# Column quarters per 32 tokens in the expert passes of a streaming encoder layer, with VectorE transposes, 16 KB weight rows and a one-hot token table

## What is computed

```python
def expert_ffn(xb, w_gu, b_gu, w_dn, b_dn):
    gu = xb @ w_gu + b_gu
    gate = jnp.minimum(gu[..., :D_FF], SWIGLU_LIMIT)
    up = jnp.clip(gu[..., D_FF:], -SWIGLU_LIMIT, SWIGLU_LIMIT)
    glu = gate * jax.nn.sigmoid(gate * SWIGLU_ALPHA)
    return ((up + 1) * glu) @ w_dn + b_dn
```

## Time and profile before

| | us |
|---|---|
| median of three runs | 1817.5 (1816.2 to 1819.22) |
| profiled execution, its own time | 1819.62 |
| span of its trace | 1817.8 |
| TensorE busy | 1570.0 (86%) |
| VectorE busy | 701.1 (39%) |
| ScalarE busy | 323.9 (18%) |
| POOL busy | 155.7 (9%) |
| mean granted TensorE clock | 0.901 |

### The profile page before, as it was taken

The page is one execution under the profiler, slowest core; times in us unless marked ns, Lnnn a source line. Parts: engine busy times, 40 slices in busy tenths (PEclk is TensorE's granted clock), DMA queues, the critical chain, the costliest instruction groups (busy, mean ns, idle before and its releaser), DMA issues.

```text
span 1817.8 us, 39267 instructions
## 1 busy us (share of the span) xinstructions
PE 1570.0 (86%) x16465; PEld 750.6 (41%) x16465; DVE 701.1 (39%) x1414; ACT 323.9 (18%) x678; POOL 155.7 (9%) x241
## 2 busy tenths in 40 slices
PE   3998888789992299999999999999999999999920
PEld 2664754555652044344443433433433433433400
DVE  1379996433346022232222222222222222222248
ACT  2231116333321011111111111111111111111001
POOL 1024104000111300000000000000000000000031
PEclk8898998655995599999999999999999999999965
DMA  9235548000444579999999999999999999997763
GB/s 346 77 106 186 186 172 300 1 4 3 151 177 156 205 310 408 402 407 401 408 406 399 396 400 390 392 403 393 391 402 392 388 409 391 393 402 272 306 249 109
DMA packets 129291, 531.20 MB, mean 292 GB/s; under 512 B 12634, under 2 KB 22156, under 8 KB 95444
## 3 DMA queue, kind: packets, MB, share of 16 engines
q1 hardware_dynamic: 100112, 472.07, 66.4%
q0 software_dynamic: 12272, 41.28, 6.9%
q10 hardware_dynamic: 16852, 17.11, 2.8%
HBM read 501.04 MB, written 29.37 MB: 292 GB/s over the span
## 4 chain that ended last, share of the span: by engine, by line
PE 50%; DMA 36%; DVE 6%; ACT 3%; issue 2%; POOL 1%; ACTq 1%; SPq 0%; DVEq 0%; POOLq 0%
DMA down_w<-in_w_down 32%; PE psum L1712 9%; PE psum L1694 8%; PE psum L1720 6%; PE psum L1515 5%; PE psum L1703 4%; PE psum L1653 3%; PE psum L1619 2%; PE psum L1523 2%; PE psum L1634 2%; DMA front_ring<-in_w_in 1%; DVE final_work L1277 1%; PE psum L1494 1%; PE psum L1627 1%; POOL slot_dram L1420 1%
## 5 line engine op out<-in xcount | busy, mean ns | idle before, releaser
L1712 PE MATMUL psum<-down_w,expert_work 128*32 128x512 f32 x2112 | 240.0, 595 | 17.2 <-DMA down_w<-in_w_down 17.2
L1694 PE MATMUL psum<-gu_even,expert_work 128*32 128x512 f32 x2176 | 239.1, 597 | 1.3 <-ACT expert_work L824 1.0
L1215 DVE TENSOR_TENSOR expert_work<-psum,expert_work 128x512 f32<-128x512 f32 x66 | 36.8, 558 | 500.6 <-PE psum L1694 372.1
L1694 PE MATMUL psum<-gu_odd,expert_work 128*32 128x512 f32 x2048 | 222.7, 592 | 0.0
L1233 DVE TENSOR_TENSOR expert_work<-psum,expert_work 128x512 f32<-128x512 f32 x66 | 36.9, 558 | 303.0 <-PE psum L1712 214.9
L1694 PEld LDWEIGHTS psum<-gu_even,expert_work 128*32 128x32 f32 x2176 | 70.9, 111 | 159.4 <-issue 156.8
L1712 PEld LDWEIGHTS psum<-down_w,expert_work 128*32 128x32 f32 x2112 | 63.0, 109 | 155.2 <-issue 120.1
L1694 PEld LDWEIGHTS psum<-gu_odd,expert_work 128*32 128x32 f32 x2048 | 66.6, 110 | 146.3 <-issue 143.6
L1703 PE MATMUL psum<-gu_even,expert_work 128*32 128x256 f32 x2176 | 124.0, 380 | 0.0
L1720 PE MATMUL psum<-down_w,expert_work 128*32 128x256 f32 x2112 | 120.0, 379 | 0.0
L1703 PE MATMUL psum<-gu_odd,expert_work 128*32 128x256 f32 x2048 | 116.8, 380 | 0.0
(11 more groups left out here) (308 smaller groups left out, 1616.9 us busy)
## 6 DMA issues: line engine op xcount, KB each, us to landing
gu_even<-in_w_gate_up SPq DMA_DIRECT2D x68, 2048.0 KB, 22.7
down_w<-in_w_down SPq DMA_DIRECT2D x66, 2048.0 KB, 23.3
gu_odd<-in_w_gate_up SPq DMA_DIRECT2D x64, 2048.0 KB, 22.9
front_ring<-in_w_mod SPq DMA_DIRECT2D x12, 2048.0 KB
ys_dram<-raw_ring POOLq DMA_DIRECT2D x1, 8448.0 KB, 39.3
ys_dram<-expert_work ACTq DMA_DIRECT2D x66, 128.0 KB, 7.2
front_ring<-in_w_in SPq DMA_DIRECT2D x4, 2048.0 KB
front_ring<-in_w_mod_final SPq DMA_DIRECT2D x4, 2048.0 KB
```

What stands on the lines that cost most here:

```text
L1215: v.tensor_tensor(eg[part], psum[:, 2 * part, 0:w], bias_of(bias_b, part, 0), ALU.add).then_inc(gu_added, 1)
L1694: last = mm(psum[32 * u:32 * u + 32, x, :], lhsT=xgT[:, k, 32 * g_:32 * g_ + 32], rhs=gu_slot(par, c)[:, k % 2, at_:at_ + WA], start=(k == ...
L1712: last = mm(psum[32 * u:32 * u + 32, 4, :], lhsT=actT[0][:, at_:at_ + 32], rhs=dn_slot(c)[:, k % 4, n * WA:(n + 1) * WA], start=(k == 0), ...
```

## The change

- The 96 tokens of a pass are three groups of 32, each as four column quarters of 256 (`gate_up` L1686, `down` L1694). For each gate/up piece TensorE takes the three groups in turn; then down for one group after another. Groups 0 and 2 share a PSUM bank for down, so group 2 waits for group 0's `rows_out`.
- The transposes are VectorE's: of tokens (L1196, 128x768) and of activations (L1213, 128x256), with weight rows laid out as `(p k)` to match: a partition's part of any 2 MB piece is one row of 16 KB.
- Tokens come by three indirect transfers of 128 rows of 1 KB (`h_quarters`). Bias loads are two instead of six, the shuffle is 768 wide.
- A pass has three stores, one per group (L814), each of 128 rows of 1 KB. `ys_dram` is seen there as quarter, token, column.
- The token table is made on the chip's engines: one-hot rows of group and place (VectorE L1175, L1178), 20 matmuls 128x153 that sum them (L1675), one drain (L1187). `slot_dram` goes.
- An overflow pass does one group of 32. gu_odd's first load no longer waits for the routing. ScalarE loads the sigmoid table once.

The core of the diff:

```diff
-        w_gu = a["w_gate_up"][0].rearrange("e (k p) n -> e p k n", p=P)
-        w_dn = a["w_down"][0].rearrange("e (k p) n -> e p k n", p=P)
+        w_gu = a["w_gate_up"][0].rearrange("e (p k) n -> e p k n", p=P)
+        w_dn = a["w_down"][0].rearrange("e (p k) n -> e p k n", p=P)
...
-            def store_rows(b):
-                act_e.wait_ge(ys_ready, 2 * b + 3)
-                for n in range(2):
-                    act_e.dma_start(ys_dram[bass.ds(b * ROWS_B, 64), n * WA:(n + 1) * WA],
-                                    ysb[0][64 * n:64 * n + 64, :]).then_inc(ys_stored, 16)
-                act_e.wait_ge(ys_ready, 2 * b + 4)
-                for u in range(GROUPS):
-                    act_e.dma_start(ys_dram[bass.ds(b * ROWS_B + 64, 32), u * WB:(u + 1) * WB],
-                                    ysb[1][32 * u:32 * u + 32, :]).then_inc(ys_stored, 16)
+            def store_rows(n, g_):
+                act_e.wait_ge(ys_ready, n + GB + 1)
+                act_e.dma_start(ys_dram[bass.ds(n * GT, GT), :].rearrange("t (u n) -> u t n", u=QUARTERS),
+                                ysb[g_]).then_inc(ys_stored, 16)
...
+                    for tt in range(T):
+                        cols = slice(TOPE * tt, TOPE * (tt + 1))
+                        v.tensor_tensor(at_group[:, cols, :], iota_g.unsqueeze(1).to_broadcast([P, TOPE, NG]),
+                                        f6[:, cols].unsqueeze(2).to_broadcast([P, TOPE, NG]), ALU.is_equal)
+                        for c in range(TOPE * tt, TOPE * (tt + 1)):
+                            ins = v.tensor_scalar(at_row[:, c, :], iota_r, f3[:, c:c + 1], tok4[:, tt:tt + 1], ALU.is_equal, ALU.mult)
+                        ins.then_inc(hot_made, 1)
...
+                elif kind == "table":
+                    for tt in range(T):
+                        pe.wait_ge(hot_made, tt + 1)
+                        rws = ROWS[tt]
+                        for c in range(TOPE * tt, TOPE * (tt + 1)):
+                            last = mm(bank(j)[:, 0:NG], lhsT=at_row[0:rws, c, :], rhs=at_group[0:rws, c, :],
+                                      start=(c == 0), stop=(c == T * TOPE - 1))
...
+            def turn_tokens(b, par):
+                dve.wait_ge(gathered, (b + 1) * (GB * 16))
+                dve.sem_inc(turn_settled, 1)
+                v.transpose(xgT[par].rearrange("p g k n -> p (g k) n"),
+                            xg.rearrange("p (g f k) -> p g k f", g=GB, k=KD)).then_inc(xgT_ready, 1)
...
+            def expert_dve(b, par):
+                turn_tokens(b + 1, 1 - par)
+                dve.wait_ge(bias_ready, b + 1)
+                for g_ in range(GB):
+                    if g_ < GB - 1:
+                        dve.wait_ge(gu_ready, b * (GB - 1) + g_ + 1)
+                    else:
+                        dve.wait_ge(gu_done, (b + 1) * GUC)
+                    gated(b * GB + g_, g_)
+                dve.wait_ge(ys_stored, (b + 1) * (GB * 16))
+                for g_ in range(GB):
+                    if g_ < GB - 1:
+                        dve.wait_ge(dn_ready, b * (GB - 1) + g_ + 1)
+                    else:
+                        dve.wait_ge(dn_done, (b + 1) * DNC)
+                    rows_out(b * GB + g_, g_)
+                spread_bias(b + 1, (b + 1) * GB)
...
+            def expert_pe(b, par, use_gu, groups, n):
+                for c in range(GUC):
+                    pe.wait_ge(gu_in[par][c], use_gu * 16 + 16)
+                    for g_ in range(groups):
+                        last = gate_up(g_, par, c, xgT[par])
+                        if g_ == groups - 1:
+                            last.then_inc(gu_done, 1)
+                        elif c == GUC - 1:
+                            last.then_inc(gu_ready, 1)
+                for g_ in range(groups):
+                    pe.wait_ge(actT_ready, n + g_ + 1)
+                    if g_ != 1:
+                        pe.wait_ge(ys_ready, n + GB + g_ // 2)
+                    for c in range(DNC):
+                        if g_ == 0:
+                            pe.wait_ge(dn_in[c], b * 16 + 16)
+                        last = down(g_, c)
+                        if g_ == groups - 1:
+                            last.then_inc(dn_done, 1)
+                    if g_ < groups - 1:
+                        last.then_inc(dn_ready, 1)
```

More of the change, by code:

```diff
@@ L123, in steps @@
             s.append(("hT", t + 1))
-    s += [("rank",)]
+    s += [("rank",), ("table",), ("over",)]
     return s
@@ L1237, in spread_bias, with rows_out @@
+            def rows_out(n, g_):
+                v.tensor_tensor(ysb[g_], down_sum(g_), bias_b[:, 2 * QW:3 * QW], ALU.add).then_inc(ys_ready, 1)
+            def spread_bias(b, rows_before):
+                dve.wait_ge(ys_ready, rows_before + GB)
                 dve.wait_ge(bias_in, (b + 1) * (BIAS_DMAS * 16))
@@ L1438, in expert_pool @@
-            def expert_pool(b):
-                pool.wait_ge(xg_turned, b + 1)
-                gather(b + 1)
-            gather(0)
+                for g_ in range(n):
+                    g.indirect_dma_start(xg[:, g_ * QW:(g_ + 1) * QW], None, h_quarters,
+                                         bass.IndirectOffsetOnAxis(idx_now[:, g_:g_ + 1], 0)).then_inc(gathered, 16)
+            in_sbuf(pool, ("table",))
+            gather(0, GB, 0)
             with pool.Fori(0, NE) as b:
-                expert_pool(b)
+                pool.wait_ge(xgT_ready, b + 1)
+                settle()
+                gather(b * GB + GB, GB, b + 1)
@@ L1698, in gate_up_rest @@
-            def gate_up_rest(par, c):
+                elif kind == "table":
+                    for tt in range(T):
[4 more added lines that the diff above has]
+                                      start=(c == 0), stop=(c == T * TOPE - 1))
+                elif kind == "over":
+                    pe.wait_ge(routed, 1)
+                    last = tr(bank(j)[0:1, 0:P], ocol, ident)
@@ L1743, in _, with down @@
-            in_sbuf(pe, ("rank",))
+                        for u in range(QUARTERS):
+                            last = mm(psum[GT * u:GT * u + GT, 2 * g_ + x, 0:QW], lhsT=xT[:, g_, k, :],
+                                      rhs=gu_slot(par, c)[:, k % 2, x * D + u * QW:x * D + (u + 1) * QW],
+                                      start=(k == 0), stop=(k == KD - 1))
+                return last
+            def down(g_, c):
+                for k in range(4 * c, 4 * c + 4):
+                    for u in range(QUARTERS):
+                        last = mm(down_sum(g_)[GT * u:GT * u + GT, :], lhsT=actT[g_][:, k, :],
+                                  rhs=dn_slot(c)[:, k % 4, u * QW:(u + 1) * QW], start=(k == 0), stop=(k == KD - 1))
+                return last
```

361 lines of the change are left out of this document (140 added, 221 removed).

## The result

| | before | changed |
|---|---|---|
| median, us | 1818.36 (1816.2 to 1819.78, 4 runs) | 1850.34 (1837.74 to 1855.36, 4 runs) |
| profiled execution, us | 1819.62 | 1837.74 |
| its span, us | 1817.8 | 1835.8 |
| start of the first expert matmul, us | 626.66 | 589.60 |
| middle passes, us each | 33.7 | 35.9 |

The change is slower: ratio 1.0167, 95% interval 1.0114 to 1.0219. The forecast was 1912 us. The time lies under the forecast's own range of 1885 to 1990 and inside the stated one only because rival 1 takes that down to 1805; the forecast growth of 94 us was three times the measured 32. The profiled execution is the fastest of the four, 12.6 us under their median, so its rows show a little less waiting than the middle one would.

The account below looks back on a forecast made before the run. The prediction took TensorE and the DMA engines as both at their limit in the experts' stage. 1817.5 - 20.7 (start) + 115.7 (passes) - 0.9 (tail) gave 1912 us; own range 1885 to 1990, low end 1805 with rival 1.

Parts of the forecast that it names:

- rival 1: Stores on four engines without the gap: they land early, only the engines' 35.5 us a pass counts; 1828 us, chance 0.16.
- Four engines for a store: Stores whose DRAM side begins with 4 column quarters use 4 engines, not 16; each gets 96 store rows a pass.
- TensorE's pass: TensorE's matmuls in a pass: 192 + 96 of 256 columns, with the ends of accumulations, take 31.4 us.
- The activation chain: Seven steps on VectorE and ScalarE per group, 3.3 us, hidden under 3.46 us of gate/up matmuls.
- A 16 KB row: Weight transfers: such a row holds its engine for 0.61 us, bounds 0.60 and 0.64.
- 34 store rows: Store rows gone per engine before weights flow again; 62 remain against 48 weight rows, so stores always land last.
- the period of 38.4 us: Time of each of 29 passes: 35.5 us of engine load plus a 3.1 us gap, less 0.2.
- the margin of 14: Store rows by which the remaining 62 exceed the next pass's 48 weight rows on the four engines.
- the term of 115.7 us: Growth of all passes together, overflow pass included: 1226.5 us against 1110.8.
- The start: Token table made on chip: expert matmuls start at 606 us, bounds 599 and 612, instead of 626.66; -20.7 us.
- the engines' own load of 35.5 us: Weight rows, 96 store rows, gathers, bias and completions on each of the four store engines, per pass.
- The rival on the other side: Stores run on all 16 engines, passes take 31.4 to 32.0 us: 1709 to 1726 us, up to 1770; chance 0.12.

Follow-up runs that it names:

- e10: The kernel before with the change's form of store (one transfer for the 64 rows, one for the 32) in place of six: 1972.66 us, ratio 1.0844.
- e3: The change with stores split by column quarter into 12 transfers a pass and TensorE's loop written out: 1728.78 us, ratio 0.949 to the kernel before.
- e1: The change with each store split into its four column quarters, 12 transfers a pass in place of 3: 1814.37 us, ratio 0.9971 to the kernel before.
- e4: The change with a second set of output buffers, a semaphore each, stores still on 4 engines: 1817.89 us, ratio 0.9986 to the kernel before.
- e5: The change with every 2 MB weight piece loaded as two transfers of 8 KB rows: 1818.95 us, ratio 1.0002 to the kernel before.
- e2: The change with TensorE's loop over pairs of passes written out 16 times: 1856.38 us, ratio 1.02 to the kernel before.
- e9: The change as it is, run once more for its spread: 1849.02 us, ratio 1.0179 to the kernel before.
- e8: The kernel before with four passes in TensorE's loop body in place of two: 1857.71 us, ratio 1.0223.
- e7: The change with two sets of output buffers and TensorE's loop written out, stores on 4 engines: 1841.24 us, ratio 1.0138 to the kernel before.
- e6: The change with stores split by column quarter, TensorE's loop written out and weights in 8 KB rows: 1740.28 us, ratio 0.9572 to the kernel before.

## Why the prediction was wrong

**What held.** Four engines for a store (18040 packets here, and e10). TensorE's pass: 31.3 us against 31.4. The activation chain is hidden: in e3 TensorE waits for nothing but down pieces, though the transposes take 655 and 1571 ns where I had 350 to 1000 and 1200. A 16 KB row is 0.61 us when nothing disturbs it (below). The direction, the mechanism (`rows_out` held by stores, TensorE's third down group behind it) and the turns row by row hold too (e1, e4, e5). The arithmetic of the range does not: the bounds named there add up to 1891 to 1998 us, not 1885 to 1990.

**The step that failed** is "By then some 34 store rows are gone; 62 remain, against 48 weight rows. So the stores always land last", and the period of 38.4 us for each of 29 passes. DMA queues of the change from 762 to 769 us, right behind the landing at 761.63, with q1 alone from 763 to 767 us as the third row; then from 769 to 776 us; then from 733 to 761 us, before that landing:

```profile
q1 hardware_dynamic: 65, 1.06, 42.4%
q10 hardware_dynamic: 264, 0.26, 12.9%
...
q1 hardware_dynamic: 16, 0.26, 26.1%
...
q1 hardware_dynamic: 199, 3.00, 100.5%
...
q1 hardware_dynamic: 674, 9.45, 87.1%
...
q10 hardware_dynamic: 287, 0.28, 2.9%
```

Right behind the landing 264 packets of q10 went out, which is 2 stores of 128 rows and 4 completions each: the stores of groups 0 and 1, all of them, 64 rows an engine and not 34. All had gone by 767, and until then q1 had started only 16 packets of weights. Only group 2's 32 rows stay for the next pass, and against 48 weight rows they land in time. (The fourth row is weights undisturbed: 3.00 MB are 183 rows, at 100.5% of 16 engines for 7 us 0.61 us each. The last two are stores under weights: 9.45 MB are 36 weight rows an engine in the mean, beside 72 store packets for each of the four, in 28 us.) That pass waits for nothing, its own stores are issued under weights, and the pass after it waits.

Two terms of that step were off. Store rows began to flow between 763 and 764 us, some 2 us after the landing, where I had 3.1. And the third down group, which frees the down pieces, was taken at 3.5 us; it took 5.35 us after 3.75 us of idle, at a lower granted clock (the 0.66 in this window, 762 to 767 us):

```profile
762.00:767.00 5.00, 4.87 (x60) 2.67 (x64) 0.41 (x2) 0.00 (x0) 0.00 (x0) 0.66 0.39 105
```

SP issued the first down load at 764.93, in the middle of that group. As an estimate, half of the extra 1.85 us gives the stores 0.9 us, or some 18 rows at 0.05 us, which alone is more than the margin of 14. No run separates the two terms: behind a third group at full clock (3.66 us) the next pass waited once (1483.23) and once did not (831.85).

The period is one of two passes. e2 shows it alone: 31.1 + 42 = some 73 us for two, 36.5 a pass, in place of 76.8. So 29 x (38.4 - 36.5) = 55 us of the term of 115.7 us are this error, by the period that e2 shows.

**What I hadn't seen** is the stop at the head of TensorE's loop. A timeline row and a window of the change:

```profile
658.58 4.05 PE L1686 MATMUL psum<-gu_even,expert_work 128*32 128x256 f32 x34 [4.74 <-issue]
...
947.00:950.00 3.00, 3.00 (x36) 1.61 (x35) 0.00 (x0) 0.00 (x0) 2.39 (x3) 0.59 0.98 416
```

4.74 us of idle before the matmul of an even pass, and the granted clock afterwards at 0.59 in the mean of 3 us, between the levels of 1.2 and 2.4 GHz: 1.9 us more for the same matmuls (22.61 against 20.72). That is 3.3 us a pass. Beside late stores it costs nothing that shows, since stores land in it: the change is at 35.9 (e9 36.3) with it, at 36.5 without (e2). With the stores mended it costs the whole: 34.7 against 32.1 us (e1, e3), 86 us of time. The loop's 15 returns go with 166 more packets of 16 KB in the instruction queue than before; e2, which never returns, has 137 more for 9216 matmuls, about 243 B each. By this estimate the body was 100 KB before, is 140 KB in the change and 200 KB in e8, and the bound lies between the first two. The Trainium skill, Runtime: NRT & Kernel Launch, section "Instruction fetch mechanics", gives TensorE a store of 128 KiB, refilled in blocks of 16 KiB, and says that a taken branch to code outside the current window of two pages has to fetch first. These runs agree with the 128 KiB: no stop at 100 KB, stops at 140 and 200. They don't agree with a window of only two blocks, which the 100 KB body would have left as well.

**The start.** I had 606 us, it was 589.60. The chain of the change (answers to the earlier trace rows):

```profile
561.17 0.87 PE psum L1666 x2
...
579.29 1.32 PE psum L1675 x8
...
585.07 2.69 DMA expert_work<-h_dram,keep
...
589.60 10.49 PE psum L1686 x161
```

From the rank matmuls to the first expert matmul it is 28.4 us, before 626.66 - 572.19 = 54.5 (the first rank matmul there, just ahead of the one in the earlier trace rows): the table gains 26 us, I had 20.7. Most of what was off is the series of table matmuls, 1.32 us for four (each leaves two records, so the row says x8), 0.33 each, where I took 0.6; they end 0.4 us behind VectorE's last one-hots. The other 11 us lie ahead of the change's work: in the twelve profiled executions of this study the first rank matmul stands anywhere from 561.2 to 574.9 us, and in those of the changed kernel and its variants at either end. So the profiled execution was an early one, by luck, and this is a part of the spread of 1%.

**The sum again**, for the profiled execution: -37 us for the start, passes from 589.60 to some 1754 = 1164 us against 1110.8, which is +54, tail +1: 1817.8 + 18 = 1835.8. The median of the change, 12.6 us above this execution, has no profile of its own; e9's profiled execution, at 1848.59 us, starts at 593.23 with 36.3 us a pass and eleven waits for `rows_out`, 41.8 us in all. Of my rivals the first came nearest (1828), but by another way: the engines' own load of 35.5 us with stores that land early. e4 shows passes of 34.65 us with the same load, so 35.5 was at least 0.8 too high (0.61 x 48 + 96 x 0.046 + 6 x 0.16 is 34.7; the gathers run as 96 packets of 4 KB a pass, 6 an engine, and not as 384 rows of 1 KB), and the stores do land late. The rival on the other side, 1709 to 1726 us with 16 engines, is what e3 reaches (1729), once the loop's stop is gone too.

## What to carry to other kernels

Read the outermost count of a transfer on both sides: here 4 in place of 32 or 64 put 3% of the traffic on four of 16 engines, and up to every second pass waited. A loop body that grows can cost its engine a stop at each return, which shows as idle time "issue" at its head and as packets in the instruction queue. When two waits fill the same time, each edit alone shows little (36 us gained and 6 lost here, 121 gained together), so try them together before one is dismissed.

## What was not expected of the hardware

- A return of TensorE's loop showed no stop with a body of 412 float32 matmuls and transposes, mostly 4.3 to 4.9 us of idle with 576, and 5.9 to 6.2 with 824; with the lower clock behind it some 6.6 and 8.5 us.
- In e7 a single store's issue on ScalarE took up to 25.1 us where the usual one takes 0.55, and held all that ScalarE had to do.
- Two queues on one engine took turns by rows (e5), so the length of the rows of one sets the wait of the other: weight rows of 8 in place of 16 KB were worth 31 us (e5) where stores were late, and cost 11.5 us (e6) where they weren't.
